# First attention: how GpSimd scales the probabilities of four heads

## The reference

```python
def sliding_window_attention(q, k, v, sinks):
    ...
    s = jnp.einsum('bnqgrd,bnkgd->bngrqk', qb, kband) * (1.0 / math.sqrt(D))
    ...
    s = jnp.where(valid[None, :, None, None], s, -jnp.inf)
    sk = sinks.astype(jnp.float32).reshape(G, R)[None, None, :, :, None, None]
    m = jnp.maximum(jnp.max(s, axis=-1, keepdims=True), sk)
    p = jnp.exp(s - m)
    denom = jnp.sum(p, axis=-1, keepdims=True) + jnp.exp(sk - m)
    p = p / denom
    o = jnp.einsum('bngrqk,bnkgd->bnqgrd', p, vband)
```

## Time and profile before

| | |
|---|---|
| median of 3 runs | 2309.35 us |
| lowest and highest | 2302.63 and 2311.84 us |
| profiled execution, first to last instruction | 2307.9 us |
| mean granted TensorE clock, share of full | 0.989 |
| first attention, units 0 to 15 | about 374 to 453 us of the span |

### The profile page before, as it was taken

The page is one execution under the profiler, slowest core; times in us unless marked ns, Lnnn a source line. Parts: engine busy times, 40 slices in busy tenths (PEclk is TensorE's granted clock), DMA queues, the critical chain, the costliest instruction groups (busy, mean ns, idle before and its releaser), DMA issues. The chain is left out here.

```text
span 2307.9 us, 29073 instructions
## 1 busy us (share of the span) xinstructions
PE 2218.0 (96%) x10136; PEld 1787.9 (77%) x10136; DVE 1617.7 (70%) x2247; ACT 1089.5 (47%) x1877; POOL 795.6 (34%) x579
## 2 busy tenths in 40 slices
PE   6999998999899999999998999999999999999998
PEld 4778887686678888888876767767778888887887
DVE  6468447626999999985797379994575555556686
ACT  5232256735644444455445368882343333334533
POOL 1030024513533232342023626661274444433310
PEclk9999999999999999999999999999999999999999
DMA  9156622033133333289944230003422333339986
GB/s 348 56 174 212 203 85 64 26 128 115 45 111 101 105 101 110 81 296 394 335 165 139 72 101 19 23 5 110 145 69 98 107 101 106 101 119 320 354 277 228
DMA packets 282565, 331.82 MB, mean 144 GB/s; under 512 B 18281, under 2 KB 180409, under 8 KB 282049
## 3 DMA queue, kind: packets, MB, share of 16 engines
q1 hardware_dynamic: 279760, 322.57, 41.4%
q0 software_dynamic: 2208, 7.37, 0.9%
q10 hardware_dynamic: 465, 0.17, 0.0%
HBM read 251.11 MB, written 78.94 MB: 143 GB/s over the span
## 5 line engine op out<-in xcount | busy, mean ns | idle before, releaser
L2643 PE MATMUL ps<-sum_hi,whi 128*128 128x512 f32 x640 | 249.5, 390 | 1.0 <-DVE wlo L2809 0.7
L2645 PE MATMUL ps<-sum_hi,wlo 128*128 128x512 f32 x640 | 249.0, 389 | 0.0
L2644 PE MATMUL ps<-sum_lo,whi 128*128 128x512 f32 x640 | 249.0, 389 | 0.0
L2669 PE MATMUL ps<-sum_lo,whi 128*128 128x512 f32 x616 | 240.7, 391 | 2.0 <-ACT arena L2754 2.0
L2671 PE MATMUL ps<-sum_lo,wlo 128*128 128x512 f32 x616 | 239.7, 389 | 0.0
L2670 PE MATMUL ps<-sum_lo,whi 128*128 128x512 f32 x616 | 239.7, 389 | 0.0
L2643 PE MATMUL ps<-hhi,whi 128*128 128x512 f32 x480 | 188.3, 392 | 9.0 <-DVE cbuf L3324 3.3
L226 DVE TENSOR_TENSOR wlo<-raw,whi 128x1024 fp32r<-128x1024 f32 x56 | 78.4, 1406 | 159.6 <-ACT whi L221 159.5
L2644 PE MATMUL ps<-hlo,whi 128*128 128x512 f32 x480 | 188.2, 392 | 0.0
L2645 PE MATMUL ps<-hhi,wlo 128*128 128x512 f32 x480 | 188.0, 392 | 0.0
L1732 POOL TENSOR_TENSOR cbuf<-cbuf,attn_stats 128x1024 f32<-128x1024 f32 x80 | 151.5, 1894 | 94.0 <-DVE attn_stats L1993 94.0
(11 more groups left out here) (450 smaller groups left out, 5575.2 us busy)
## 6 DMA issues: line engine op xcount, KB each, us to landing
shared<-ffn_blocks SPq DMA_DIRECT2D x154, 256.0 KB, 5.1
lead_work<-in_w_down SPq DMA_DIRECT2D x105, 256.0 KB, 4.4
arena<-in_w_down SPq DMA_DIRECT2D x100, 256.0 KB, 4.1
raw<-in_w_up SPq DMA_DIRECT2D x36, 512.0 KB, 5.1
ffn_blocks<-chunk_work SPq DMA_DIRECT2D x66, 256.0 KB, 2.3
ffn_blocks<-lead_work SPq DMA_DIRECT2D x66, 256.0 KB, 2.3
raw<-in_w_in SPq DMA_DIRECT2D x32, 512.0 KB, 4.7
arena<-in_w_ada SPq DMA_DIRECT2D x32, 512.0 KB, 5.5
```

What stands on the lines that cost most here:

```text
L2643: nc.tensor.matmul(o, hi[:, ws], mhi, start=fresh and k == 0, stop=False, skip_group_check=True)
L2644: nc.tensor.matmul(o, hi[:, ws], mlo, start=False, stop=False, skip_group_check=True)
L2645: mm = nc.tensor.matmul(o, lo[:, ws], mhi, start=False, stop=(k == 3), skip_group_check=True)
L2669: nc.tensor.matmul(o, hi[:, ws], mhi, start=fresh, stop=False, skip_group_check=True)
```

## The change

In the first attention the one GpSimd multiplication of a 128x1024 tile is replaced. Its second operand was the four reciprocals, each spread over 256 columns. Now there are four operations of 128x256, each with one reciprocal for each partition as its scalar operand. The last of the four counts the semaphore. The second attention keeps its single multiplication, written for one factor alone.

GpSimd's blocks of the first attention are written out one after the other and no longer use the hardware loop. The other engines keep theirs.

```diff
                         for e in range(per_n):
                             u, sl = unit(n, e), e % 2
                             pool.wait_ge(S["recip"], u.val(add=1))
-                            q = 1 if full else 4
-                            p = prob[sl].rearrange("p (r k) -> p r k", k=T // q)
-                            nc.gpsimd.tensor_tensor(p, p, st[:, sl, 16:16 + q].unsqueeze(2).to_broadcast([P, q, T // q]),
-                                                    ALU.mult).then_inc(S["scaled"], 1)
+                            if full:
+                                p = prob[sl].unsqueeze(1)
+                                nc.gpsimd.tensor_tensor(p, p, st[:, sl, 16:17].unsqueeze(2).to_broadcast([P, 1, T]),
+                                                        ALU.mult).then_inc(S["scaled"], 1)
+                            else:
+                                for r in range(4):
+                                    p = prob[sl][:, r * wk:(r + 1) * wk]
+                                    ins = nc.gpsimd.tensor_scalar(p, p, st[:, sl, 16 + r:17 + r], None, ALU.mult)
+                                ins.then_inc(S["scaled"], 1)
...
-                    query_blocks(pool, ahead, body)
                     if full:
+                        query_blocks(pool, ahead, body)
                         lead.pool_last(pool)
                         following.pool(pool)
+                    else:
+                        ahead()
+                        for i in range(NB):
+                            body(At(i), i + 1 < NB)
```

## The result

The changed kernel takes **2324.72 us** (median of 4 runs, 2318.26 to 2326.07). The kernel before, measured beside it, takes 2308.3 us (4 runs, 2302.63 to 2311.84). The ratio is 1.0076, with a 95% interval of 1.0057 to 1.0094: slower by 0.6 to 0.9%, where I had forecast no change. The profiled span grew from 2307.9 to 2324.3 us, by 16.4.

The account below looks back on a forecast made before the run. TensorE and ScalarE were taken to bound the first attention, with GpSimd's scaling hidden in steady units. Only unit 0 gained, 0.4 us: span 2307.9 to 2307.5 us, forecast median 2309 us (no change), range 2303 to 2314.

Parts of the forecast that it names:

- What bounds the kernel: First attention: TensorE and ScalarE fill the 8.20 us pair of units; GpSimd, busy 4.33 us, isn't last in steady units.
- the price of the added operation: GpSimd scaling, first attention: four 128x256 operations, priced like one-input copies, take 1.5 us where one took 1.89.
- my high end: Upper bound for the four GpSimd scalings: each scalar read like a second tensor, 2.40 us in all.
- my 1.41: Low end for the four GpSimd scalings, if the scalar costs nothing: 3 x 0.34 + 0.39 = 1.41 us.
- The 0.34 us that I estimated for four small reads: GpSimd scaling: possible extra for four operations if each scalar is a small read command of about 102 cycles.
- The room: First attention's steady units: GpSimd's scaling may last up to about 1.89 + 0.35 = 2.24 us without delaying the transposes.
- Rival 2: GpSimd scaling: four operations slow one by one, 5.1 us, paid in each unit; 46 us more, 2355 us; chance 0.05.
- threshold of 3.0 us: GpSimd scaling: length of four operations, 0.75 us each, from which the kernel would be measurably slower, by 11.5 us.
- Rival 1: GpSimd scaling: scalar as dear as a tensor, 2.40 us for four; 2.7 us more, 2312 us; chance 0.15.
- rival 4: GpSimd scaling: four operations take the 1.89 us of the one; time stays 2309 us; chance 0.02.
- Rival 3: First attention: GpSimd gated more than said, 4.4 us of weight-load waits come back; 2305 us; chance 0.10.
- The chance of slower: Whole kernel: probability 0.05 of a measurable slowdown, against 0.93 for same and 0.02 for faster.

Follow-up runs that it names:

- e4: Changed kernel with GpSimd's blocks still written out, but the scaling again one 128x1024 operation with spread reciprocals: 2306.33 us, ratio 1.0001 to the kernel before.
- e6: Changed kernel, each of the four operations given a second step, adding 0.0 after multiplying by the reciprocal: 2306.79 us, ratio 1.0002 to the kernel before.
- e7: Changed kernel, the four operations multiply by the constant 1/32 and add 0.0, no reciprocals read: 2307.9 us, a single run.
- e2: Changed kernel, the four operations multiply by the constant 1/32 in one step, no reciprocals read: 2325.52 us, ratio 1.0080 to the kernel before.
- e3: Changed kernel, each of the four operations multiplies by its reciprocal spread over the columns as a tensor: 2310.22 us, ratio 1.0011 to the kernel before.
- e5: Changed kernel with eight one-step operations of 128x128, two for each head, in place of four of 128x256: 2345.03 us, a single run.

## Why the prediction was wrong

**What bounds the kernel: right.** The written-out blocks cost nothing (e4), the scalings of 1.81 to 1.89 us all leave the pair at 8.20 to 8.22 us (e4, e6, e7), and in e6 the transposes' matmuls wait for VectorE seven times, 3.6 us, and for GpSimd never. A scaling much shorter than 1.8 us was not run.

**The step that failed is the price of the added operation.** I wrote that "a tensor-by-scalar operation with constants belongs to this family" of copies, on the row of 1008 columns. That row is of an operation with two steps, which the source line shows, and the new one has one. By e2 and e7, the same constant and the same tile take 0.848 us with one step and 0.405 with two. I took 1.5 us for four and it was 3.63. The bound was wrong with it: my high end, 2.40 us, was the price of a tensor operand, which e3 measured at 2.33. I took it for granted that a scalar can't cost more than a tensor. Even the right form misses my 1.41: four take 1.84 us, because one starts every 0.45 us and not every 0.34. The 0.34 us that I estimated for four small reads did not appear: with reciprocals four take 1.84 us (e6), with constants 1.81 (e7).

**The room was 2.16 us, not 2.24.** This is a small error. I had taken 0.35 us from unit 5; my reading of unit 6, 0.26 us for the first half, would have given 2.15.

**How often it is paid.** Rival 2 has the right sign, and its threshold of 3.0 us was passed. Its sum with the measured 3.63 us would be (3.63 - 2.24) x 15 + 1.74 = 22.6 us, where the span grew by 16.4. I had counted each unit, and it is each pair. Counted so, seven pairs of 1.47 make 10.3 us. The stretches between the starts of the scalings give the whole loss of the stage:

| from unit to unit | before, us | clock | after, us | clock | loss, us |
|---|---|---|---|---|---|
| 0 to 2 | 6.96 | 0.52 | 10.10 | 0.61 | 3.14 |
| 2 to 4 | 9.31 | 0.99 | 12.19 | 0.86 | 2.88 |
| 4 to 6 | 8.23 | 1.00 | 9.67 | 1.00 | 1.44 |
| 6 to 8 | 8.23 | 1.00 | 9.70 | 1.00 | 1.47 |
| 8 to 10 | 8.20 | 1.00 | 11.30 | 0.85 | 3.10 |
| 10 to 12 | 8.15 | 1.00 | 10.14 | 1.00 | 1.99 |
| 12 to 14 | 8.22 | 1.00 | 11.04 | 0.94 | 2.82 |
| 14 to 15 | 4.27 | 1.00 | 5.97 | 0.83 | 1.70 |

What is lost beyond 1.47 us a pair is 8.2 us. Four stretches have a lower clock than before (2 to 4, 8 to 10, 12 to 14, 14 to 15); in 2 to 4 the slow operation of 1.81 us accounts for an estimated 0.9 of it. In 0 to 2, 10 to 12 and 12 to 14 GpSimd, with its copies and squares, is busy for 9.8 to 11.0 us and hardly ever idle, so its own work bounds them. How the 8.2 us divide between the clock and GpSimd isn't shown.

**Rival 2's mechanism was another.** It rested on the row of 1.93 us. In the same trace VectorE ran `wlo<-raw,whi`, two inputs from SBUF, from 1287.96 for 1.22 us, which covers the start of that operation. The fast row has a neighbour too, but there GpSimd began first, at 1303.15: it took 1.03 us, and VectorE's `arena<-arena`, from 1303.22, took 2.03. So the 0.90 us belong most likely to the neighbour on VectorE and are no price of the instruction; no run took the neighbour away. Nothing in the stage paid it four times.

```profile
1287.96 1.22 DVE L226 TENSOR_TENSOR wlo<-raw,whi 128x1024 fp32r<-128x1024 f32 x1 [9.30 <-ACT whi L221]
```

**Rival 1** (the scalar as dear as a tensor) and **rival 4** gave no measurable change and fell. **Rival 3** was hardly tested: e6 shortens the scaling by only 0.05 us. The waits for GpSimd put down to the weight loads fell there from 4.4 to 3.3 us, and the ratio is 1.0002. The chance of slower, 0.05, was too small. A kind of operation that the trace had never shown carried the whole sum, and I bounded it by what looked like it.

## What to carry to other kernels

Price an operation by a row with the same steps and the same operand kinds, not by its name alone; read the source line of the row. On GpSimd, write a lone multiplication by a scalar as a multiplication and an addition of zero: on fp32 in SBUF, in place, four of 128x256 take 1.84 us and not 3.63. When an engine with slack gets longer, find the circle of waits that it would close and how often that is run, here once for two units.

## What the runs showed of the hardware

- GpSimd's tensor-by-scalar operation with one step takes 2.50 ns a column and 0.29 us fixed (0.605, 0.926 and 2.848 us at 128, 256 and 1024 columns). With two steps and constants it took 0.405 us at 256 and 1.03 at 1008, which is 0.83 ns a column and 0.19 us fixed. The Trainium skill, GPSIMD Engine Reference, section 4.1, says that one-input operations on GpSimd run roughly at line rate. The trace agrees for two steps, which cost what a copy costs for each column, and disagrees for one, three times dearer. Why one step is slower isn't known from these runs.
- In the last unit of the changed kernel the third of the four operations took 2.50 us, from 460.28. VectorE's two operations with both inputs in SBUF, 2.37 us in all, ran at that time:

```profile
458.48 5.20 POOL L1737 TENSOR_SCALAR cbuf<-cbuf,attn_stats 128x256 f32<-128x256 f32 x4 [1.09 <-DVE attn_stats L2002]
```

```profile
459.70 2.37 DVE L2207 TENSOR_TENSOR hlo<-arena,hhi 128x1024 fp32r<-128x1024 f32 x2
```

  The four took 5.20 us and not 3.63. In e6 they took 3.86 and not 1.84 beside the same pair. The Trainium skill, SBUF — State Buffer, under "Who interferes with whom", says that such a VectorE instruction contends with a GpSimd instruction that reads SBUF, and that the second to issue waits. The trace agrees for GpSimd, which began while VectorE's first was running; no run took VectorE's two operations away. It doesn't agree for VectorE: its first began at 459.70, inside GpSimd's second operation (459.38 to 460.31), and took 1.23 us, where the same operation took 1.21 before with GpSimd idle (389.14). Beside GpSimd's copies VectorE did wait: the 128x4 addition in `reciprocals` took 1.54 us at 386.62, until the copy ended at 388.16, and 0.16 at 379.70, in the middle of a scaling.
- Longer waits of TensorE went with a lower clock, though not each time. Before, the pairs from unit 4 on ran at a granted clock of 1.00. In the changed kernel a pair in which TensorE had waited 1.93 us for GpSimd ran at 0.85 and took 11.30 us beside 9.70. Its eight transposes took 1.94 us, where they take 1.09 at full clock:

```profile
423.79 1.94 PE L1899 MATMUL ps<-identF,cbuf 128*128 128x128 f32 x8 [1.93 <-POOL cbuf L1737]
```

  A pair with a wait of 2.15 us ran at 1.00, so the length of one wait alone doesn't tell it. In e5, with longer waits still, two pairs ran at 0.86.
